# Rows of maxima and inverse denominators in the mLSTM stage, as stacked high and low parts

## The reference, cut to what matters

```
log_d = where(causal, b[..., :, None] - b[..., None, :] + lic[..., None, :], -inf)
m_row = maximum(log_inter, max(log_d))
s   = (q k^T) * exp(log_d - m_row[..., None])
den = inter * (q n) + sum(s)
h   = num / maximum(abs(den), exp(-m_row))[..., None]
```

## Time and profile before

| what | value |
|---|---|
| median of 3 runs | 2583.51 us (2581.18 to 2583.63) |
| the profiled execution, its own time | 2579.49 us |
| its span, first to last instruction | 2577.5 us |
| PE busy | 2497.7 us (97%) |
| DVE, ACT, POOL busy | 47%, 38%, 38% |
| mean granted clock of TensorE | 0.988 |
| mLSTM stage | about 1345 to 2190 us |

### The profile page before, as it was taken

One profiled execution on the slowest core, in us unless ns is written; L12 is line 12 of the kernel. 1 busy time (PEld: TensorE's weight loads), 2 busy tenths in 40 slices (PEclk: granted clock), 3 DMA queues, 4 the chain that ended last, 5 costly groups with the idle time before them and its releaser, 6 DMA issues.

```text
span 2577.5 us, 32394 instructions
## 1 busy us (share of the span) xinstructions
PE 2497.7 (97%) x12482; PEld 2023.1 (78%) x12482; DVE 1206.1 (47%) x2190; ACT 987.7 (38%) x1731; POOL 978.6 (38%) x512
## 2 busy tenths in 40 slices
PE   9998999999999899999999999999999999899998
PEld 6886788888788678888888777878787787887776
DVE  4356589530235647974025421521241242546664
ACT  5455344432255535444333223121222222455552
POOL 3322355765432225576653223222222223322231
PEclk9999999999999999999999999999999999999999
DMA  4211244222321123532331111111111111110100
GB/s 175 72 46 66 90 169 183 98 92 96 114 66 62 50 82 139 196 115 94 107 117 57 50 34 64 42 41 66 50 57 34 49 58 42 53 66 25 32 27 33
DMA packets 54584, 200.48 MB, mean 78 GB/s; under 512 B 6176, under 2 KB 6176, under 8 KB 53664
## 3 DMA queue, kind: packets, MB, share of 16 engines
q1 hardware_dynamic: 52272, 189.27, 21.3%
q10 hardware_dynamic: 2160, 9.15, 1.0%
HBM read 196.29 MB, written 2.10 MB: 77 GB/s over the span
## 4 chain that ended last, share of the span: by engine, by line
PE 78%; DVE 15%; ACT 3%; issue 2%; POOL 2%; DVEq 0%; ACTq 0%; POOLq 0%
PE ps L868 25%; PE ps L540 18%; PE ps L560 16%; PE ps L590 11%; DVE arena L1936 7%; DVE arena L2129 1%; PE ps L759 1%; DVE arena L2126 1%; DVE norm_sq L1900 1%; PE ps L1182 1%; POOL norm_acc L2582 1%; POOL wl L2569 1%; PE ps L775 1%; DVE hl L1912 1%; PE ps L986 1%
## 5 line engine op out<-in xcount | busy, mean ns | idle before, releaser
L2569 POOL TENSOR_TENSOR wl<-wring,wh 128x1024 fp32r<-128x1024 f32 (+1 forms) x305 | 770.9, 2528 | 1257.9 <-ACT wh L1222 1246.5
L1222 ACT ACTIVATE wh<-wring 128x1024 fp32r<-128x1024 f32 (+1 forms) x305 | 317.1, 1043 | 556.4 <-PE ps L868 318.6
L540 PE MATMUL ps<-hh,wh 128*128 128x512 f32 x768 | 300.0, 391 | 9.8 <-DVE hl L1912 5.1
L540 PE MATMUL ps<-hh,wl 128*128 128x512 f32 x768 | 299.1, 389 | 0.0
L540 PE MATMUL ps<-hl,wh 128*128 128x512 f32 x768 | 299.0, 389 | 0.0
L590 PE MATMUL ps<-arena 128*128 128x512 f32 (+2 forms) x912 | 266.8, 429 | 15.5 <-ACT arena L1449 5.5
L590 PEld LDWEIGHTS ps<-arena 128*128 128x128 f32 x912 | 143.0, 193 | 100.7 <-issue 77.5
L560 PE MATMUL ps<-hh,wh 128*128 128x512 f32 (+1 forms) x472 | 202.3, 429 | 4.9 <-DVE hl L2550 2.4
L560 PE MATMUL ps<-hh,wl 128*128 128x512 f32 (+1 forms) x472 | 189.4, 401 | 0.0
L560 PE MATMUL ps<-hl,wh 128*128 128x512 f32 (+1 forms) x472 | 189.0, 400 | 0.0
L1936 DVE CUSTOM_DVE_ANT_0 arena<-arena 128x1024 f32<-128x1024 f32 x96 | 182.6, 1902 | 8.6 <-DVE arena L2129 0.3
(11 more groups left out here) (334 smaller groups left out, 5242.0 us busy)
## 6 DMA issues: line engine op xcount, KB each, us to landing
wring<-wts SPq DMA_DIRECT2D x290, 512.0 KB, 3.3
arena<-wts SPq DMA_DIRECT2D x48, 512.0 KB, 4.1
wring<-wts SPq DMA_DIRECT2D x16, 384.0 KB, 2.9
xL<-xt SPq DMA_DIRECT2D x4, 512.0 KB, 5.3
arena<-tab SPq DMA_DIRECT2D x1, 2048.0 KB, 15.6
arena<-cv ACTq DMA_DIRECT2D x2, 1024.0 KB, 5.0
arena<-tab ACTq DMA_DIRECT2D x1, 2048.0 KB, 7.9
out_t<-xL ACTq DMA_DIRECT2D x8, 256.0 KB, 2.1
```

What stands on the lines that cost most here:

```text
L540: mm = nc.tensor.matmul(o[0], a, b, start=start and k == first and j == 0, stop=stop and k == last and j == 2)
L1222: nc.scalar.activation(wh[:, sn % SPLIT_SLOTS, :kn * w], raw(u)[:, :kn * w], ACT.Copy).then_inc(act_done, tick("act", ("hi", u)))
L2569: G.tensor_tensor(wl[:, sn % SPLIT_SLOTS, :kn * w], raw(u)[:, :kn * w], wh[:, sn % SPLIT_SLOTS, :kn * w].bitcast(F32), ALU.subtract).then_inc(
```

## The change

The maxima and the inverse denominators are now kept in two new fp32r buffers of 128 x 768, `mxr` (named mx_rows in the trace) and `rrr` (rr_rows). Partitions 0 to 35 hold the part rounded to fp32r, partitions 64 to 99 the rest, and all others zero. A small buffer `pick8` holds, for each of the 8 pairs of head and direction, a column with a one at both the high and the low row. One fp32r product over 100 rows with that column as the weight then yields high plus low on all partitions. Buffers move: `rrr` lies where `acc[1]` was, which is read for the last time before; `emr` lies in the table of parameters, over columns that are no longer read; the scan of the maxima is written to `gates["t1"]`.

```diff
-        mmx, emr = cut(MMX, TA)[0:36], cut(MMX, TA)[64:100]
+        mxr = place("mx_rows", TA, F32R, ar + MMX)[0]
+        rrr = place("rr_rows", TA, F32R, nsq_off + TA)[0]
+        pick8 = place("pick8", 8, F32R, ar + PICK)[0]
+        emr = prmt[0:36, PC["conv"]:PC["conv"] + TA]
@@ max_rows
+                pe.wait_ge(dve_done, at("dve", "pick8"))
                 claim_pair(0, "act", "e", h, d, NA - 1)
-                r = ROW0[d] + h
-                pick = idn[0:36, r:r + 1].to_broadcast([36, P])
+                pick = pick8[0:100, 4 * d + h:4 * d + h + 1].to_broadcast([100, P])
                 c, l = wide(0, 0, P)
-                nc.tensor.matmul(c, pick, mmx[:, 0:TC], start=True, stop=True)
-                chain(l, [(pick, mmx[:, TC:TA])], ("mb", h, d))
+                nc.tensor.matmul(c, pick, mxr[0:100, 0:TC], start=True, stop=True)
+                chain(l, [(pick, mxr[0:100, TC:TA])], ("mb", h, d))
@@ weight_rows
-                    nc.tensor.matmul(c, pick, acc[0][0:36, 0:TC], start=True, stop=True)
-                    chain(l, [(pick, acc[0][0:36, TC:TA])], ("rb", h, d))
+                    nc.tensor.matmul(c, pick, rrr[0:100, 0:TC], start=True, stop=True)
+                    chain(l, [(pick, rrr[0:100, TC:TA])], ("rb", h, d))
@@ DVE, gates
-            V.memset(mmx, 0.0).then_inc(dve_done, tick("dve"))
+            V.memset(mxr[:].bitcast(F32), 0.0).then_inc(dve_done, tick("dve"))
...
-            directions(mmx, a, ALU.max, ALU.max)
-            V.tensor_tensor(fm[0:36], f[0:36], mmx, ALU.add).then_inc(dve_done, tick("dve"))
+            mx = gates["t1"]
+            directions(mx, a, ALU.max, ALU.max)
+            V.tensor_tensor(fm[0:36], f[0:36], mx[0:36], ALU.add).then_inc(dve_done, tick("dve", ("gfm",)))
+            V.tensor_scalar(mxr[0:36], mx[0:36], -1.0, None, ALU.mult).then_inc(dve_done, tick("dve"))
+            V.tensor_tensor(pick8[:, 0:4], idn[:, 0:4], idn[:, 64:68], ALU.add).then_inc(dve_done, tick("dve"))
+            V.tensor_tensor(pick8[:, 4:8], idn[:, 32:36], idn[:, 96:100], ALU.add).then_inc(dve_done, tick("dve"))
             dve.wait_ge(dve_done, now("dve"))
-            V.tensor_scalar(mmx, mmx, -1.0, None, ALU.mult).then_inc(dve_done, tick("dve", ("gfm",)))
+            V.scalar_tensor_tensor(out=mxr[64:100], in0=mx[0:36], scalar=-1.0, in1=mxr[0:36].bitcast(F32),
+                                   op0=ALU.mult, op1=ALU.subtract).then_inc(dve_done, tick("dve", ("pick8",)))
@@ DVE, inverse_rows
                 V.tensor_tensor(q, den, q, ALU.max).then_inc(dve_done, tick("dve", ("q", h)))
+                V.memset(rrr[:].bitcast(F32), 0.0).then_inc(dve_done, tick("dve"))
                 dve.wait_ge(dve_done, now("dve"))
-                V.reciprocal(q, q).then_inc(dve_done, tick("dve", ("rr", h)))
+                V.reciprocal(q, q).then_inc(dve_done, tick("dve"))
+                dve.wait_ge(dve_done, now("dve"))
+                V.tensor_copy(rrr[0:36], q).then_inc(dve_done, tick("dve"))
+                dve.wait_ge(dve_done, now("dve"))
+                V.tensor_tensor(rrr[64:100], q, rrr[0:36].bitcast(F32), ALU.subtract).then_inc(
+                    dve_done, tick("dve", ("rr", h)))
```

More of the change, by code:

```diff
@@ L163 @@
 HCH, HCL, XC, HN, MQK, MV = 0, 2048, 4096, 6144, 12288, 15360
-ED, EX, MMX, ACOL, SGZ, SEL = 18432, 22016, 23808, 24576, 24800, 25568
+ED, EX, MMX, ACOL, SGZ, SEL, PICK = 18432, 22016, 23808, 24576, 24800, 25568, 25664
 NC, NF = 22528, 23552
```

## The result

The changed kernel takes 2558.97 us (median of 4 runs, 2555.06 to 2562.72) against 2582.35 us for the kernel before in its runs so far (4, 2574.44 to 2583.63): a ratio of 0.9920, 95% interval 0.9900 to 0.9939, 0.8% faster. Forecast were 2562.8 us and a range of 2557 to 2571. Two later comparisons of the same two kernels gave 0.9923 (0.9909 to 0.9937) and 0.9911 (0.9895 to 0.9926). The profiled execution took 2555.06 us, with a span of 2553.0.

A forecast was written before the change was run, and what follows sets the result against it. PE was taken to bound the kernel. Savings of 10.6 us (maxima) and 9.0 (inverse denominators), together 19.7, plus 1 for the clock made 20.7 us off the median 2583.51: 2562.8 us, range 2557 to 2571.

The forecast's parts named there:

- What bounds it: mLSTM stage: PE is busy 843.57 of 845.00 us, so what is taken from PE is taken from the end.
- rival C: Later stages: the saved time is given back there as PE waits longer; 2580 to 2584 us, chance 0.05.
- The products: `max_rows` saves 1.33 us in each of 8 calls, `weight_rows` 2.26 in each of 4: together 19.7 us.
- Rival A, only the passes: Both edited places: idle steps around the products stay, only three of four passes go; 16.8 us saved, 2566.7, chance 0.08.
- Rival B, the repeated column's load: New products: weight loads show, 0.19 us for each of 32, 6 us; 13.7 saved, 2569.8 us, chance 0.05.
- The clock: Behind the last `weight_rows`: the dip to 1.2 GHz goes with the fp32 pairs; 0 to 4 us, taken as 1.
- DVE's cost: Ahead of the loop and in each head: DVE's added work is covered by slack and costs 0.
- my two courses: `inverse_rows` tail on DVE: 2.3 to 2.7 us added if unhindered, up to 4.8 if held by POOL.
- the plain sum: Each head on DVE, without POOL: memset 0.70, cast 0.55 to 0.95, subtraction 0.95, waits 0.1; 2.3 to 2.7 us.
- my rule of two inputs: `inverse_rows` on DVE: an instruction with two SBUF inputs is blocked in full by POOL reading SBUF, so the subtraction can be held.
- Rival D, the threshold: `weight_rows`, four times: PE waits for DVE's tail; the change loses from 12.4 us of added tail; 2594 at 15, chance 0.02.
- The time: Whole kernel: 20.7 us less than the median of 2583.51, so 2562.8 us, range 2557 to 2571.

The follow-up runs named there:

- The halves: Changed kernel with only the maxima single-pass: 2572.23 us, ratio 0.9962; with only the inverse denominators single-pass: 2569.55 us, ratio 0.9959.
- the single pair put back: Changed kernel with the second direction's inverse denominators spread by the old fp32 products again: 2567.31 us beside 2582.78 for the kernel before.

## Why the prediction was right, point by point

- *What bounds it, and rival C.* Right: PE is busy in all of the stage before and after, and what was taken from it (21.3 us) appeared at the end in full, with the stretch behind unchanged (429.0 and 428.9 us). So nothing was given back later.
- *The products.* Right to 0.01 us: 0.81 and 1.04 us against 0.81 and 1.05, so 8 x 1.33 + 4 x 2.27 = 19.7. The halves show it apart: 10.7 us for the maxima.
- *Rival A, only the passes.* Wrong by 3 us of 19.7, as shown by the full change and by the single pair put back (1.34 against 1.05). The Trainium skill (FP8 and Floating Point Precision, TensorE Precision Notes) gives four passes for true FP32; the fp32 pair agrees (1.48 us from 1472.27 to 1473.75 against 4 x 0.35), and the steps at its edges come on top.
- *Rival B, the repeated column's load.* No trace of it: 0.12 us from the start of the 256-column product to the next (1466.71 to 1466.83), as in the projections.
- *The clock.* The direction was right and the size was low: I took 1 us of a possible 4; it was 1.6, with one spell in each of three traces. My reading that fp32 pairs of 36 rows bring it fits the eleven traces without waits for `weight_rows`, though only as two things that come together; behind `max_rows`, a single pair with projections on both sides, no trace has a spell. Why it is one of the four calls, and not always the same, stays open.
- *DVE's cost.* Right at nothing, and near the dearer of my two courses: I put the tail between 2.3 and 4.8 us and the rows at latest 2.7 us ahead of PE; it was 4.3 us and they came 3.2 us ahead. I had the cast at 0.55 to 0.95 us in the plain sum; held by POOL it is 2.58 us, in all four heads. The Trainium skill (SBUF — State Buffer, Who interferes with whom) counts casts among those that can take the port pair shared with GpSimd; here it was the cast that was held in the full change (2.58), and it was free in the kernel with one reciprocal more (0.55). The subtraction, at which my rule of two inputs pointed, came behind POOL's low part and took its plain 0.95 us.
- *Rival D, the threshold.* The direction was right, the point wrong: I took each us of overshoot for one us of time and put the break-even at 12.4 us of tail. With two reciprocals, a tail of 12.2 us, the wait was 21.6 us in all and the loss 31.0. By that ratio the 21.3 us that the stage gained are used up by about 21.3 x 21.6 / 31.0 = 15 us of wait in all, not by 21: an estimate of 7.5 + 15 / 4 = 11 us of tail. What I left out is that PE works at 1.2 GHz for a while behind a wait.
- *The time.* 2562.8 forecast, 2558.97 measured. How near the median came is in part luck: three medians of the changed kernel are 2558.97, 2562.05 and 2554.68 us. The spans of the profiled executions differ by 24.5 us where 20.7 were forecast: 0.6 of the rest is the clock in the stage, and 3.1 lie ahead of it, where the kernels do the same work and the clock sum is 15.5 us before and 10.2 after.

## What to carry to other kernels

A product that only spreads rows is cheap to make single-pass, if the rows are split in two parts stacked on free partitions; take its price from start to start across its neighbours, since the change of kind costs too. Before adding DVE work on the way to such a product, read the slack at that place: with 7.5 us it cost nothing, even when 7.3 of them were used; beyond, each us of waiting cost 1.4 to 1.6; with no slack the added work took back all or nearly all of the gain, and moving the product behind half a tile of other work gave most of it back. Where single executions scatter as much as the effect, cut the traces at instructions that both kernels share.

## What the runs showed of the hardware

- A cast of 4 rows of 512 columns and one of 36 rows of 768 both took about 2.5 us (2.41, 2.58) when they met a POOL subtraction, and the larger took 0.55 us when it met none.
- PE's granted clock fell although PE was busy in the whole slice (5.00 of 5.00 us at 0.66, and 0.73 in the second trace), right behind fp32 products of 36 rows. It cost 1.6 to 1.7 us in each of three traces.
- Waits of 2.3 us on average made PE lose some 1.9 us more behind three of four; waits of 5.4 us lost 2.3 us more behind each. In all the stage paid 1.6 and 1.4 us for each us of waiting.
